# Large products in plain float32: no high and low parts, weights used as they land in nine buffers, seven block products in all k pairs of the down projections

## The reference

```python
u = rmsnorm(x, norm_mix_g) @ w_in                 # 1024 -> 5376
merged = g_a * (o_a @ w_proj_a) + g_b * (o_b @ w_proj_b)
x = x + merged @ w_out
x = x + jnp.square(jax.nn.relu(h @ w_ff1)) @ w_ff2
...
def swiglu(x, w_gate, w_up, w_down):
    return (jax.nn.silu(x @ w_gate) * (x @ w_up)) @ w_down
```

## Time and profile before

| what | value |
|---|---|
| time of the runs | 1415.37 us median of 3 (1415.28 to 1415.47) |
| the profiled execution | 1415.34 us, of which the span shown is 1413.4 us |
| PE busy | 1406.8 us, 100% of the span |
| PEld busy | 1197.1 us |
| DVE busy | 1179.5 us, 83% |
| ACT busy | 819.2 us, 58% |
| granted TensorE clock | 1.00 |
| DMA | 249.12 MB, mean 176 GB/s |

### The profile page before, as it was taken

The page is one execution under the profiler, slowest core; times in us unless marked ns, Lnnn a source line. Parts: engine busy times, 40 slices in busy tenths (PEclk is TensorE's granted clock), DMA queues, the critical chain, the costliest instruction groups (busy, mean ns, idle before and its releaser), DMA issues.

```text
span 1413.4 us, 22918 instructions
## 1 busy us (share of the span) xinstructions
PE 1406.8 (100%) x9197; PEld 1197.1 (85%) x9197; DVE 1179.5 (83%) x1641; ACT 819.2 (58%) x1103; POOL 26.5 (2%) x93
## 2 busy tenths in 40 slices
PE   9999999999999999999999999999999999999999
PEld 8988778888888888889878888888888887888887
DVE  6876786898877898998868988988889798688897
ACT  7735474565447555555766665555555557665562
POOL 0000000000001100000000000000000000000000
PEclk9999999999999999999999999999999999999999
DMA  8441236555554555455434555545555453355543
GB/s 335 155 151 62 101 110 208 173 185 203 194 221 179 185 203 185 173 208 192 141 118 172 185 195 187 213 169 197 200 179 197 165 177 148 112 201 195 180 177 119
DMA packets 36105, 249.12 MB, mean 176 GB/s; under 512 B 4128, under 2 KB 4256, under 8 KB 6688
## 3 DMA queue, kind: packets, MB, share of 16 engines
q1 hardware_dynamic: 35712, 247.46, 49.4%
q10 hardware_dynamic: 288, 0.19, 0.1%
HBM read 246.59 MB, written 1.05 MB: 175 GB/s over the span
## 4 chain that ended last, share of the span: by engine, by line
PE 97%; DMA 1%; ACT 1%; DVE 0%; issue 0%; SPq 0%; DVEq 0%; ACTq 0%
PE ps L2219 24%; PE ps L2131 16%; PE ps L2133 15%; PE ps L2132 15%; PE ps L2226 13%; PE ps L2393 2%; PE ps L2203 1%; PE ps L2207 1%; PE ps L2209 1%; DMA raw<-ws 1%; PE ps L2307 1%; PE ps L2606 1%; PE ps L2586 1%; PE ps L2595 1%; PE ps L2378 0%; ACT hi L2649 0%
## 5 line engine op out<-in xcount | busy, mean ns | idle before, releaser
L3017 DVE TENSOR_TENSOR lo<-raw,hi 128x2048 fp32r<-128x2048 f32 (+1 forms) x230 | 525.0, 2283 | 60.3 <-ACT hi L2649 57.6
L2649 ACT CAST hi<-raw 128x2048 fp32r<-128x2048 f32 (+1 forms) x230 | 439.8, 1913 | 186.6 <-PE ps L2133 118.9
L2219 PE MATMUL ps<-h,hi 128*128 128x512 f32 x1504 | 359.0, 390 | 0.0
L2219 PEld LDWEIGHTS ps<-h,hi 128*128 128x128 f32 x1504 | 276.4, 188 | 52.5
L2131 PE MATMUL ps<-hi,a 128*128 128x512 f32 x516 | 205.0, 397 | 0.0
L2133 PE MATMUL ps<-hi,a 128*128 128x512 f32 x516 | 201.4, 390 | 0.0
L2132 PE MATMUL ps<-lo,a 128*128 128x512 f32 x516 | 201.2, 390 | 0.0
L2226 PEld LDWEIGHTS ps<-h,lo 128*128 128x128 f32 x1504 | 192.2, 190 | 7.9
L2226 PE MATMUL ps<-h,lo 128*128 128x256 f32 x1504 | 194.4, 282 | 0.0
L2846 ACT COPY a<-ps 128x256 f32<-128x256 f32 x208 | 76.1, 373 | 143.5 <-PE ps L2219 78.5
L2131 PEld LDWEIGHTS ps<-hi,a 128*128 128x128 f32 x516 | 96.9, 188 | 22.6 <-issue 2.4
(11 more groups left out here) (383 smaller groups left out, 1800.1 us busy)
## 6 DMA issues: line engine op xcount, KB each, us to landing
raw<-ws SPq DMA_DIRECT2D x229, 1024.0 KB, 4.8
X<-xin SPq DMA_DIRECT2D x8, 256.0 KB, 5.3
raw<-ws SPq DMA_DIRECT2D x2, 512.0 KB, 6.5
out<-X SPq DMA_DIRECT2D x4, 256.0 KB, 2.2
small<-small SPq DMA_DIRECT2D x1, 992.5 KB, 12.8
const<-const SPq DMA_DIRECT2D x1, 900.0 KB, 6.8
a<-row SPq DMA_DIRECT2D x1, 512.0 KB, 6.2
const<-const SPq DMA_DIRECT2D x1, 388.0 KB, 13.2
```

What stands on the lines that cost most here:

```text
L2219: t = e.matmul(b2(s["slots"][u]), wh[:, k, 128 * u:128 * u + 128], h2[:, k, :, :], start=k == 0, stop=last)
L2649: e.copy(hi[j % NSPL][:, n], raw[j % NRAW][:, n]).then_inc(hi_ready, 1)
L3017: e.tensor_tensor(lo[j % NSPL][:, n], raw[j % NRAW][:, n], hi[j % NSPL][:, n].bitcast(F), ALU.subtract).then_inc(lo_ready, 1)
```

## The change

- Every large product takes plain `F` operands: one `matmul` in the program where there were three (or two wide ones). The splits of weights and activations, on ACT and DVE, go, with their semaphores.
- The weights are used from `raw`. The space of `hi` and `lo` goes to six more buffers: `NRAW` 9, `load` of piece i+9 waits for the last product of piece i.
- `SEVENS` lists all 9 pairs of each SwiGLU's down projection and 14 of `w_ff2`: 50 pieces, with three sets of sums.
- The planner's costs of large products are 0.43 for 512 columns and 0.215 for 256.
- The sums of the stick-breaking attention (`sb_sum`) and the forget gate's product (`fg_mm`) become plain as well. The zeros for `warm` move to `VN`, an `F` tile.

```diff
-NRAW = 3
-NSPL = 3
+NRAW = 9
-SEVENS = {"a": (1, 3, 4, 6, 7), "s": (3, 5, 7, 9, 11)}
+SEVENS = {"a": (0, 1, 2, 3, 4, 5, 6, 7, 8), "s": (0, 1, 2, 3, 4, 5, 6, 7, 8, 9, 10, 11, 12, 13)}
+SUM_SETS = 3
...
-        hi = [fixed(f"hi{i}", [128, PIECE], R) for i in range(NSPL)]
-        lo = [fixed(f"lo{i}", [128, PIECE], R) for i in range(NSPL)]
-        zeros = lo[NSPL - 1][:, 0:512]
...
+        zeros = VN[:, 0, :]
...
-            emit("wide" if wide else "cols", pe=FINE * 0.36, i=i, a=j + 128 * u, o=u, k0=k, nk=nk, src=src, slot=slot,
+            emit("cols", pe=FINE * 0.215, i=i, a=j + 128 * u, o=u, k0=k, nk=nk, src=src, slot=slot,
...
-            emit("rows", pe=3 * 0.227, i=i, b=b, c=cut, k=k, kt=kt, per=per, src=src, slot=slot, opens=opens,
+            emit("rows", pe=0.43, i=i, b=b, c=cut, k=k, kt=kt, per=per, src=src, slot=slot, opens=opens,
...
-                    o = b2(sl)[:, s["o"], :]
                     a = s["a"]
                     for k in range(s["k0"], s["k0"] + FINE):
-                        t = mm3(o, wh[:, k, a:a + 128], wl[:, k, a:a + 128], sh[:, k, :], sl_[:, k, :],
-                                k == 0, k == nk - 1)
+                        t = e.matmul(b2(sl)[:, s["o"], :], w[:, k, a:a + 128], acts_of[s["src"]][:, k, :],
+                                     start=(s["o"], k) == (0, 0), stop=(s["o"], k) == (1, nk - 1))
...
-                    t = mm3(banks[sl.b][:, :], sh[:, s["kt"], tok], sl_[:, s["kt"], tok], wh[:, s["k"], c], wl[:, s["k"], c],
-                            s["opens"], s["closes"])
+                    t = e.matmul(banks[sl.b][:, :], acts_of[s["src"]][:, s["kt"], 128 * s["b"]:128 * s["b"] + 128],
+                                 w[:, s["k"], s["c"]:s["c"] + 512], start=s["opens"], stop=s["closes"])
...
-                    t = mm3(banks[sl.b][:, :], ah, al, wh, wl, s["opens"], s["closes"])
+                    t = e.matmul(banks[sl.b][:, :], a, b, start=s["opens"], stop=s["closes"])
...
-                    e.copy(hi[j % NSPL][:, n], raw[j % NRAW][:, n]).then_inc(hi_ready, 1)
...
-                e.tensor_tensor(lo[j % NSPL][:, n], raw[j % NRAW][:, n], hi[j % NSPL][:, n].bitcast(F),
-                                ALU.subtract).then_inc(lo_ready, 1)
...
+                elif kind == "load":
+                    i = s["j"] % NRAW
+                    e.wait_ge(s["after"][0], s["after"][1])
+                    e.dma_start(raw[i][:, :], ws[s["j"]]).then_inc(raw_in[i], 16)
```

More of the change, by code:

```diff
@@ L502, in sums_of @@
             src, unit = sevens[j]
-            return by_src[src].sums[unit % len(by_src[src].sums)]
+            return by_src[src].sums[unit % SUM_SETS]
         sevens = {}
@@ L607, in program @@
[L607 to L664, removed]
+        def load_behind(i, slot=None):
+            freed[i] = (full[slot.b], slot.f) if slot else (used.sem, used.add())
+            next_piece[0] += 1
+            if i + NRAW < len(plan):
+                emit("load", j=i + NRAW, after=freed[i])
+        def sums_next(n=1):
+            for _ in range(n):
+                j = next((j for j in sorted(sevens) if j not in seven_at), None)
+                if j is None:
+                    return
+                own = [wsum_v.add() for _ in range(3)]
+                seven_at[j] = own[-1]
+                emit("w_sums", dve=2.6, j=j, own=own, used=sum(x < j for x in sevens) - min(sevens[j][1], SUM_SETS - 1))
@@ L706, in cols_piece @@
             nk, w = plan[i][3], plan[i][5]
-            yield from split(i)
             for j in range(0, w, 256):
@@ L727, in wide_piece @@
-        def wide_piece(name, layer, c, needs, begin, evac):
-            piece_check(name, layer, 0, c)
-            i = next_piece[0]
-            yield from split(i)
-            sls = []
-            for u in range(2):
-                yield from room(1)
-                sls.append(take())
-                for k in range(0, 8, FINE):
-                    cols_step(i, 0, u, k, 8, "h", sls[u], needs, True)
-                    if k + FINE < 8:
-                        yield "pe"
-                begin(sls[u], c, u)
-                if u == 1:
-                    piece_done(i, sls[1])
-                    if not evac(sls[1], c, i + NSPL, sls[0]):
-                        for sl in sls:
-                            give(sl)
-                yield "pe"
@@ L749, in wide_runs @@
-        def wide_runs(name, layer, c, needs, begin, evac):
-            piece_check(name, layer, 0, c)
-            i = next_piece[0]
-            yield from split(i)
-            yield from room(2)
-            sls = [take(), take()]
-            cur[0] = max(cur[0], lo_due[i])
-            emit("wide_runs", pe=5.56, i=i, slots=sls, hi_last=runs[0] % 2 == 1, need=unmet(needs(7)))
-            runs[0] += 1
-            for u in range(2):
-                begin(sls[u], c, u)
-            piece_done(i, sls[1])
-            if not evac(sls[1], c, i + NSPL, sls[0]):
-                for sl in sls:
-                    give(sl)
-            yield "pe"
@@ L768, in program, with cols_two @@
[L768 to L774 removed]
+        def cols_two(jobs, needs):
+            i0 = next_piece[0]
+            sls = []
             def out(n):
[L777 to L780 removed]
+                jobs[n][3](sls[n], jobs[n][2])
+                give(sls[n])
             for half in range(2):
[L783 removed]
+                for n, (name, layer, c, evac) in enumerate(jobs):
@@ L853, in seven_piece @@
                 if n == 0:
-                    need.update(lo=(lo_ready, i + 1), own=unmet(needs(k + 1, 0)), mixed=unmet((mix_v.sem, mixed[k])))
+                    need.update(raw=(raw_in[i % NRAW], 16 * (i // NRAW + 1)), own=unmet(needs(k + 1, 0)),
+                                mixed=unmet((mix_v.sem, mixed[k])), second=unmet((wsum_v.sem, seven_at[i] - 2)))
                 if n == first_sum:
                     need.update(sums=unmet((wsum_v.sem, seven_at[i])))
-                apart = which in "1567"
-                emit("seven", i=i, which=which, k=k, src=src, unit=unit, slot=slots[which], opens=apart and opens,
-                     closes=apart and closes, frees=which == "4", uses=n == 6, need=need)
+                sl = slots[which]
+                emit("seven", pe=0.43, i=i, which=which, k=k, src=src, unit=unit, slot=sl, opens=sl.b not in opened,
+                     closes=which in "1567" and closes, frees=which == "4", uses=n == 6, need=need)
+                opened.add(sl.b)
                 yield "pe"
@@ L1201, in weave @@
             dry = 0
-            while pool or not all(x["serves"] for x in live):
+            while pool or live:
                 while pool and sum(x["pooled"] for x in live) < depth:
@@ L2267, in tensor_program @@
                 elif kind == "seven":
-                    j = s["i"] % NSPL
                     if s["opens"]:
                         claim(sl)
-                    for who in ("lo", "own", "mixed", "sums"):
+                    for who in ("raw", "own", "mixed", "second", "sums"):
                         if s["need"].get(who):
```

747 lines of the change are left out of this document (166 added, 581 removed).

## The result

| | before | changed kernel |
|---|---|---|
| median | 1415.32 us, 4 runs (1415.12 to 1415.47) | 1704.7 us, 4 runs (1704.36 to 1705.17) |
| ratio to before | 1 | 1.2045 (95% interval 1.2024 to 1.2066) |

A forecast was written before the change was run, and what follows sets the result against it. TensorE was taken to bound the kernel: 1413.4 + 284.0 (large products) + 3.2 (stick-breaking sums) + 0.5 (forget gate) + 4 (start) = 1705.1 us of span, with 1.9 us around it 1707 us. Range 1685 to 1745 us.

The forecast's parts named there:

- What bounds the kernel: Whole kernel before: TensorE, busy 1406.8 of 1413.4 us, bounds it; VectorE's and ScalarE's splits, 965 us, are hidden.
- Two records for a plain product: Large products: each plain float32 product is recorded as two TensorE instructions, some 3800 of 256 columns and 1676 of 512.
- Its price: Large products: a plain one takes 0.854 us for 512 columns and 0.43 for 256, against 0.68 and 0.36 before.
- The start: Eight warming products on zeros become plain: transposes begin 5.1 us later, net +4 us after waits that go.
- Sevens: Down projections: 25 further pieces with seven products instead of eight save 25 x 0.854 = 21 us.
- Stick-breaking sums: Stick-breaking attention: twelve `R` products, 1.31 us, become six plain ones, 1.71 us; eight such sums, +3.2 us.
- Costed at nothing: Loads, nine buffers, weight sums, late `seven_add` and halved planner costs add no wait; up to 15 us as mixer bound.
- The rest of TensorE: TensorE outside the large products: sums +3.2 us, forget gate +0.5, start +4; everything else stays.
- Rival (a): Large plain products cost half, 0.43 us for 512 columns and 0.215 for 256: about 965 us; chance 0.04.
- Rival (b): Long rows of plain products cost 14 to 17 ns more per record: +80 us, 1785 us; chance 0.06.
- Rival (c): New waits in mixers and attention layers from the half-priced plan, or from VectorE with `seven_add`: 1725 to 1760 us; chance 0.10.
- the time with one float32r product: Kernel before with high by high alone: expected 785 to 900 us, TensorE's whole work 592 us and no longer bounding.

## Why the prediction was right

1707 us was forecast and 1704.7 measured. The steps:

- **What bounds the kernel.** Right, and by more than the trace of before: 449 us off VectorE change the time by 2.2 us, and a kernel with all of the old work on both engines is as slow as the changed one.
- **Two records for a plain product.** Right, 3808 and 1676 records, as reckoned from the mixer's few.
- **Its price.** 0.43 and 0.854 us were taken; 0.432 and 0.86 is what long rows take. Over 1904 and 838 products that is 7 to 9 us more than the 1534.4 us of the sum.
- **The start.** The transposes were to begin 5.1 us later and do so 5.6 us later (10.60 against 5.02). The first large product is 4.55 us later; net +4 was taken. The prediction let the slower level end with the zeros at 5.02 us; it went on to 6.2, over five transposes.
- **Sevens.** 21 us reckoned, 22.2 measured.
- **Stick-breaking sums.** +3.2 us was taken for eight of them. The attention has four: their 48 records took 5.3 us before and 7.1 after, +1.8.
- **Costed at nothing.** Loads and buffers (four do as nine), the planner's costs (1.1 us), the late `seven_add` (no wait of PE on it) and the weight sums: right.
- **The remainder.** With the measured price and start the sum would be some 8 us higher, and yet the span is 1.8 us shorter than the 1705.1 reckoned. So about 10 us were saved that no term has. The two traces say where, if each product on TensorE is charged with the time from its start to the start of the next. The large products before took 1274 us, not the 1250.4 of the sum, and after they took 1549, not 1534.4. They grew by 275 us instead of 284. The sum had left out the places where large and small products change. An `R` product behind a small one took 97 ns more than in a long row, and one before a small one 48 more (124 and 123 places, 17.8 us). For plain large products it is 34 and 36 ns (108 and 107 places, 7.4 us). The prediction allowed 8 us for that in its range and none in its sum.
- **The rest of TensorE.** Everything but the large products grew by 15.3 us, where 7.7 was taken. In it are the 4.55 of the start, the 1.8 of the sums, the new wait of 1.7, and about 4 for the small products right before a large one, which took 148 ns each instead of 98; the rest, some 3 us, is the forget gate and what I can't assign. So one miss of 9 us too much and one of 8 us too little nearly cancel. That the total came within 2.3 us is in part luck; the mechanism and the two prices are not.

Rival (a), half the price, is out by every count above. Its condition, a product of 512 columns under 0.68 us, is missed by 0.18. Rival (b) is out by the narrower records. Rival (c), new waits, came to a single one of 1.7 us in the mixer, against its 20 to 55: PE idles as long as before in all, and true costs give 1 us. The Trainium skill's rule against this change (page "FP8 and Floating Point Precision", section TensorE Precision Notes: four passes for true float32) came out near, as one plain product of 512 columns is 3.8 of the 0.227 us that an `R` product takes. The half rate that the Trainium skill's page "Perfetto Trace Analysis", section Engine Utilization, gives is what one record shows (0.43 us for 512 columns); for a product it must be counted twice.

The clear miss was an expectation behind the prediction, the time with one float32r product. I took the casts and the chains of the mixers for more hidden than they are once TensorE has a third of its large columns left, and I reckoned its work at the full clock (592 us; it was busy for 697). The zeros in `R` were a smaller miss, 3.3 us for 5 to 6.

## What to carry to other kernels

When one engine is full, work moved off the others pays next to nothing, however many hundred microseconds it is: first price what the change does on the full engine, in distance from one instruction to the next, and count the places where kinds of product change, for each has a price. Before an instruction is swapped for another kind, find that kind somewhere in the old trace and count records against the source: here "one product for three" was 0.86 us for 0.68, visible in two products of a group norm. And when a cheaper instruction does empty the full engine, expect to stop well short of its gain, since the covered chains surface (979 us with TensorE busy for 697).

## What the runs showed of the hardware

- A plain float32 product stands as two instructions on TensorE, each 0.216 us for 256 columns or 0.43 us for 512, with 128x128 weights that change with every product; halving the width costs 3.2 ns a further record. A float32r product is one, 0.227 us for 512 columns and 0.12 for 256.
- At the start, with TensorE idle before, its products stood twice as far apart as later: 0.43 us instead of 0.227 for an `R` product of 512 columns, 0.85 instead of 0.43 for one record of a plain one, 0.213 instead of 0.109 for a transpose's record. In each of the eleven traces this ended with the first record of the granted clock, at 4.4 to 7.6 us (6.2 before, 5.9 in the changed kernel). Asked for the stretch before that, the view of the profile still prints a granted clock of 1.00, since no record lies there; here the distances tell more than that figure.
- A change between a large and a small product costs both sides something. Before, the large `R` products lost 17.8 us to 124 such visits to small ones and back, and the plain ones of the changed kernel 7.4 us to 108.
- The granted clock of TensorE fell to 0.86 (mean of a stretch) where it was busy for 68% of the time with gaps of a few us, and was 1.00 from its first record to TensorE's last product in the traces of the two kernels that kept it full. I had not expected it: the estimate for that run was made at full clock.
